# Three tiles instead of four beside the paged attention, token groups of 384 and 424, and a chunk inverse that multiplies half the columns

## The chip, the cores and the metric

The kernel runs on one core of a Trainium2 chip. The metric is the device time of one execution in microseconds, taken as the median of several runs. All arithmetic is in 32-bit floats. The engines are PE (matrix), DVE (vector), ACT (scalar), POOL (GpSimd), and SP, which here only issues DMA. PEld is PE's loading of weights. Each engine works through its own instruction list in order.

## The reference

One decoder layer for a prompt of 2048 tokens and a sample batch of 8 sequences of 4 tokens (32 rows, so 2080 tokens in all), width 1024. Cut to what matters here:

```
cols = rmsnorm(x) @ w_in           # columns split among three head groups
x += w_out @ concat[ GatedDeltaNet (6 heads of 64) | DiffAttention (4 heads of 64) | RWKV7 (6 heads of 64) ]
x += memory cross attention (4 heads of 128, 256 memory tokens)
x += ConvGLU: w_out @ (silu(causal conv3(gate)) * val),  gate, val = rmsnorm(x) @ w_in  (2816 each)
y = rmsnorm(x)
```

GatedDeltaNet works in chunks of 64 tokens: `a_mat` is strictly lower triangular, and `(a_mat + I)` has to be solved against `v` and `k` before the state is carried on. RWKV7 is a step by step recurrence on a 64x64 state per head; the kernel brings it to the same chunked form with a triangular inverse. The sample rows' DiffAttention reads a paged cache: 8 sequences x 64 pages x 128 positions of K and V, 512 pages each of 128 KB, found through a page table. The outputs are the final activations, the new K/V rows, and all states.

## The kernel before

`build` is a series of stages; within one stage several "lanes" run beside each other. A lane is one generator for each engine, and each `yield` in it is a slot. `weave` (L234) interleaves lanes by `(i + 0.5) / n` of slot i of n; `merge` (L243) interleaves them by places written out for each slot. The order it gives is the order in which the instructions stand in each engine's list, so an instruction that waits holds all of its engine's work behind it, whichever lane that is from.

The stages in order: `front` (norm, Q, K, V), then the input projection beside the prompt's DiffAttention, then the **paged stage**, then the sample rows' recurrences and the memory projection, then the **dense stage**, then the small outputs.

In the paged stage `paged_lanes` (162 slots: 16 for each of 8 sequences, 32 more for the last ones' remains, two others) runs beside the first LEAD = 4 tiles of 128 prompt tokens of `gdn_lanes` (24 slots a tile) and after them of `rwkv_lanes` (25 slots a tile), joined by `in_turn`. A third lane on SP, `states`, loads constants and states. In each of the first 128 paged slots PE flips one group of four K pages (L1190) for `score`; K has a ring of six groups, all loaded in the first slot on SP (L1136), one more each slot after that. V has a ring of seven groups of four pages, three pages issued by POOL and one by ACT, and is applied four groups at a time (L1249), at slots 5, 8, 11 and 14 of the sequence after. The last application is paged slot 143 in the lane's own count.

In the dense stage `feed_lanes` takes the 2080 tokens in NCH = 5 groups of CH = 416 (`op` output projection, `ns` norms, `wq`, `sc`, `tp`, `pv`, `wo` memory attention, `fg`, `fv`, `fo` feed-forward, `ft` turning back for the store; 129 slots a group). The other 12 tiles of both recurrences run beside it, three to a group in groups 0 to 3, spread over the first 0.92 of the group. SP waits in `tokens_done` for the tiles that the next group needs. The sample rows' memory attention, `memory_lanes`, runs beside group 4, which has no recurrence tile.

A recurrence tile has the slots `pre` to `RV` (GDN: to `X0`), then the chunk inverse, then `KS`, `SA`, `OD` for each of its two chunks, `post` and `back`. The inverse is `Scan64`. It keeps the inverse X and its transpose XT for 6 heads and 2 chunks of 64, and doubles the size of the inverted blocks at each of five levels b:

- slot `Y{b}`: `left` makes 12 products AM_b x X on PE, and ACT copies them to Y;
- slot `W{b}`: `right` makes 12 products for X (not at level 5) and 12 for XT, and DVE subtracts them from X and XT;
- POOL prepares the masked matrices AM_b.

All of these are 64x64 times 64x64, the two chunks in the two halves of the partitions. Each matmul stands in the trace as two instructions.

## Time and profile before

| | |
|---|---|
| median of 3 runs | 5926.58 us (5918.99 to 5926.8) |
| profiled execution | 5921.17 us, its span 5919.5 us |
| PE busy | 5294.7 us, 89% |
| PEld busy | 3261.9 us, 55% |
| DVE, ACT, POOL busy | 2368.5, 1498.2, 784.4 us (40, 25, 13%) |
| mean granted clock of PE | 0.917 of full speed |
| DMA | 487.80 MB, mean 82 GB/s |
| paged stage | about 1365 to 2180 us |
| dense stage | about 2440 to 5900 us |

Busy times are unions of an engine's instructions. The granted clock is the share of full speed that PE was given. A wait is idle time of an engine ahead of an instruction, with what ended it. The columns of the stage views are: stretch, its length, then busy time and number of instructions of PE, PEld, DVE, ACT and POOL (engines without such instructions are left out when one tile's name is asked for), PE's granted clock, the busy share of the DMA engines, and GB/s.

### The profile page before, as it was taken

What the parts mean: (1) busy time and instruction counts of PE and PEld (TensorE: products, weight loads), DVE (VectorE), ACT (ScalarE), POOL (GpSimd) and SP (SyncE); (2) the same over time, 40 slices, a digit from 0 to 9 for tenths busy, and PEclk for the clock granted to TensorE, in tenths of its full rate; (3) what the DMA queues carried; (4) which work ended last, traced back from release to release, by engine and by line L of the source; (5) the groups of instructions that cost most, each with busy time, mean ns of one, the idle gap of its engine ahead of it and who ended that gap; (6) DMA issues with size and microseconds to landing.
All of it is one profiled execution on the core that took longest, in us unless ns stands there. A gap on an engine that the chain in (4) does not pass through costs nothing. (4 is left out here: it accounts for less than half of the span.)

```text
span 5919.5 us, 91242 instructions
## 1 busy us (share of the span) xinstructions
PE 5294.7 (89%) x34908; PEld 3261.9 (55%) x34908; DVE 2368.5 (40%) x5479; ACT 1498.2 (25%) x3418; POOL 784.4 (13%) x1063
## 2 busy tenths in 40 slices
PE   8988999995777756889999899998999999989998
PEld 5644445554555542565555655565555655657554
DVE  1156655543445436253433534335333443321322
ACT  2235443432223210121212212122122221211212
POOL 0012221111443310110001101011010110100000
PEclk9989999997987855889999899998999989998998
DMA  3111011104776620312223122232233122241332
GB/s 97 48 31 36 29 33 35 35 32 137 227 223 193 181 70 9 105 43 72 86 72 102 51 73 84 77 84 62 73 87 93 54 76 74 75 130 51 95 94 69
DMA packets 729154, 487.80 MB, mean 82 GB/s; under 512 B 78058, under 2 KB 704106, under 8 KB 728687
## 3 DMA queue, kind: packets, MB, share of 16 engines
q1 hardware_dynamic: 677457, 393.53, 23.3%
q0 software_dynamic: 18432, 50.36, 2.9%
q10 hardware_dynamic: 32832, 38.09, 1.9%
q8 instruction: 278, 4.55, 0.3%
q14 instruction: 155, 1.27, 0.1%
HBM read 432.76 MB, written 49.09 MB: 81 GB/s over the span
## 5 line engine op out<-in xcount | busy, mean ns | idle before, releaser
L3368 PE MATMUL s_f_b<-s_f_h,s_f_W 128*128 128x416 f32 x4480 | 1640.8, 522 | 31.1 <-DMA s_f_h<-o_t 22.1
L3368 PEld LDWEIGHTS s_f_b<-s_f_h,s_f_W 128*128 128x128 f32 x4480 | 845.8, 192 | 708.7 <-issue 691.3
L3426 PE MATMUL s_f_b<-s_f_a,s_f_W 128*128 128x416 f32 x1760 | 634.1, 516 | 0.2
L536 PE MATMUL s_p_acc<-s_hT,s_p_W 128*128 128x416 f32 x1600 | 626.3, 539 | 6.9 <-DMA s_p_W<-in_w_in_dram 6.9
L3426 PEld LDWEIGHTS s_f_b<-s_f_a,s_f_W 128*128 128x128 f32 x1760 | 328.5, 190 | 263.5 <-issue 257.4
L536 PEld LDWEIGHTS s_p_acc<-s_hT,s_p_W 128*128 128x128 f32 x1600 | 300.1, 196 | 286.2 <-issue 269.5
L3624 DVE TENSOR_TENSOR s_f_xT<-s_f_xT,s_f_b 128x416 f32<-128x416 f32 x160 | 93.5, 586 | 587.1 <-PE s_f_b L3426 533.3
L3645 POOL TENSOR_TENSOR s_f_ex<-s_f_ex,s_f_mix 128x416 f32<-128x416 f32 x105 | 111.8, 1065 | 1348.9 <-ACT s_f_mix L3454 1348.3
L918 ACT ACTIVATE s_prob<-s_s_ps,s_ntop 128x512 f32<-128x512 f32 (+3 forms) x320 | 196.4, 619 | 368.2 <-DVE s_ntop L969 368.0
L3497 ACT ACTIVATE s_f_raw<-s_f_b 128x416 f32<-128x416 f32 x110 | 56.9, 517 | 774.9 <-PE s_f_b L3368 774.9
L1165 POOL DMA_DIRECT2D s_V<-in_cache_diff_v_dram x384 | 207.6, 541 | 278.5 <-issue 274.9
L966 DVE TENSOR_REDUCE s_ntop<-s_s_ps 128x2 f32<-128x1024 f32 (+3 forms) x160 | 169.9, 1062 | 62.8 <-PE s_s_ps L866 60.5
L3557 DVE TENSOR_SCALAR s_f_mix<-s_f_raw,s_f_taps,s_f_bias 128x416 f32<-128x416 f32 (+1 forms) x110 | 56.7, 516 | 321.8 <-ACT s_f_raw L3497 160.5
L1190 PE MATMUL s_tp<-s_ident,s_K 128*128 128x128 f32 x1024 | 162.9, 309 | 24.1 <-DMA s_K<-in_cache_diff_k_dram 17.6
L3507 ACT ACTIVATE s_f_val<-s_f_b 128x416 f32<-128x416 f32 x110 | 56.8, 516 | 444.1 <-PE s_f_b L3368 444.1
L866 PE MATMUL s_s_ps<-s_kT,s_qT 32*128 32x512 f32 (+3 forms) x640 | 163.4, 587 | 0.0
L1190 PEld LDWEIGHTS s_tp<-s_ident,s_K 128*128 128x128 f32 x1024 | 129.7, 158 | 41.2 <-DMA s_K<-in_cache_diff_k_dram 18.8
L1046 POOL TENSOR_SCALAR s_prob<-s_prob,s_alpha 128x512 f32<-128x512 f32 (+3 forms) x160 | 103.2, 660 | 275.5 <-DVE s_alpha L996 272.8
L1365 DVE COPY s_kT<-s_tp 128x512 f32<-128x512 f32 x128 | 88.2, 689 | 126.1 <-PE s_tp L1190 125.2
L1310 ACT ACTIVATE s_kT<-s_tp 128x512 f32<-128x512 f32 x128 | 75.9, 593 | 219.3 <-PE s_tp L1190 217.2
L1249 PE MATMUL s_o_ps<-s_V,s_PT 128*32 128x256 f32 x1024 | 82.0, 475 | 55.1 <-DMA s_V<-in_cache_diff_v_dram 55.0
L3171 POOL TENSOR_TENSOR s_g_zg<-s_g_zt,s_norm_g 128x384 f32<-128x384 f32 x16 | 16.0, 997 | 850.6 <-DVE s_g_o L3051 805.4
(790 smaller groups left out, 8010.0 us busy)
## 6 DMA issues: line engine op xcount, KB each, us to landing
s_f_W<-in_ffn_w_in_dram SPq DMA_DIRECT2D x220, 512.0 KB, 3.9
s_K<-in_cache_diff_k_dram SPq DMA_DIRECT2D x512, 128.0 KB, 2.9
s_V<-in_cache_diff_v_dram POOLq DMA_DIRECT2D x384, 128.0 KB, 3.2
s_f_W<-in_ffn_w_out_dram SPq DMA_DIRECT2D x80, 448.0 KB, 3.8
cols_t<-s_p_out ACTq DMA_DIRECT2D x100, 208.0 KB, 1.9
s_f_W<-in_w_out_dram SPq DMA_DIRECT2D x40, 512.0 KB, 4.6
s_f_W<-in_ffn_w_out_dram SPq DMA_DIRECT2D x40, 512.0 KB, 4.1
s_V<-in_cache_diff_v_dram ACTq DMA_DIRECT2D x128, 128.0 KB, 3.3
```

Source lines behind the costliest of these rows:

```text
L536: mm = pe.matmul(self.acc[n % 2][:, 0:CH], self.W[:, u, k, :], self.hT[:, k, c * CH:(c + 1) * CH], start=(k == 0), stop=(k == KD - 1))
L866: mm = pe.matmul(s_ps[hh][:, m, 0:wd], qT[r:r + 32, b, i * P:(i + 1) * P], kT[r:r + 32, b, 512 * c:512 * c + wd], start=True, stop=True)
L918: e = act.activation(prob[:, slot(n, c), r, 0:wd], s_ps[hh][:, m, 0:wd], ACT.Exp, scale=scale, bias=ntop[:, u, c, r:r + 1], accum_out=den[ ...
L966: dve.tensor_reduce(ntop[:, u, c, 2 * hh:2 * hh + 2], s_ps[hh][:, :, 0:wd], AX.X, ALU.max)\
L1046: m = pool.tensor_scalar(prob[:, k, 2 * hh + 1, 0:wd], prob[:, k, 2 * hh + 1, 0:wd], alpha[:, n % 2, c, 2 * hh + 1:2 * hh + 2], 1.0, ALU.m ...
L1165: pool.dma_start(V_[:, g % VG, i, :], vp[page_of(pool, g, i)].rearrange("a p h d -> p (a h d)"))\
L1190: mm = pe.transpose(dst[:, i, :], K[:, g % KG, i, h * P:(h + 1) * P], pr.ident[:, :])
L1365: dve.tensor_copy(kT[:, g % 6, 1, :], src[:, :, :].rearrange("p i n -> p (i n)"))\
L3368: mm = pe.matmul(bank(u)[:, 0:G], w[:, k, :], h[:, k, :], start=(k == 0), stop=(k == KD - 1 and kind != "op"))
L3426: mm = pe.matmul(bank(u)[:, 0:G], w[:, k, :], a[:, f % NA, :], start=(k == 0), stop=(k == len(part) - 1))
L3624: dve.tensor_tensor(xT[:, m, :], xT[:, m, :], bank(u)[:, 0:G], ALU.add).then_inc(E.sem[kind + "k"], 1)
L3645: pool.tensor_tensor(acc, acc, sq[:, m % 2, :], ALU.add).then_inc(E.sem["add"], 1)
```

## The change

Four edits that go together:

1. LEAD goes from 4 to 3: three tiles of each recurrence run in the paged stage, 13 in the dense stage.
2. The token groups are 384, 424, 424, 424 and 424 instead of five of 416. Group 0 needs exactly three tiles. `spread` gives each group the tiles that the next one needs: four pairs in group 0 and three in groups 1 to 3. The quarters of a group are 96 or 106 tokens.
3. `Scan64` multiplies only the half of the columns that a level changes: of each pair of blocks of 2^b columns `left` reads the left half of X, `right` the left half of Y and the right half of XT. The products stand packed in the PSUM bank (32 columns a head), and ACT's copy and DVE's subtractions work on 192 elements a partition instead of 384. The 64x64 operand that is loaded as weights stays whole.
4. Y gets a home of its own with a slice for each level, zeroed once by POOL, since only half of its columns are written: 1,920 elements a partition. In the paged stage it lies in the tile that later holds the memory's K and V, and both recurrences use it in turn.

```
-LEAD = 4
+LEAD = 3
+GROUPS = (384, 424, 424, 424, 424)
+GROUP_AT = tuple(sum(GROUPS[:c]) for c in range(len(GROUPS)))
+GROUP_P = GROUPS[-1] - NS
...
+    def side(self, x, r, h, b, right):
+        return x[r, h, :].rearrange("p (k a s) -> p k a s", a=2, s=2 ** b)[:, :, right, :]
+
+    def sides(self, x, b, right):
+        return x.rearrange("p h (k a s) -> p (h k) a s", a=2, s=2 ** b)[:, :, right, :]
+
+    def cell(self, bank, r, h, b):
+        return bank[r, h * HD // 2:(h + 1) * HD // 2].rearrange("p (k s) -> p k s", s=2 ** b)
+
+    def cells(self, bank, b):
+        return bank[:, 0:W_A // 2].rearrange("p (k s) -> p k s", s=2 ** b)
...
     def left(self, pe, bank, b):
         for h, r in self.each():
-            mm = pe.matmul(self.view(bank)[r, h, :], self.AM[b % 2][r, h, :], self.X[r, h, :], start=True, stop=True)
+            mm = pe.matmul(self.cell(bank, r, h, b), self.AM[b % 2][r, h, :], self.side(self.X, r, h, b, 0),
+                           start=True, stop=True)
         return mm
...
-                pe.matmul(self.view(bank_x)[r, h, :], self.XT[r, h, :], self.Y[r, h, :], start=True, stop=True)
-            mm = pe.matmul(self.view(bank_xt)[r, h, :], self.Y[r, h, :], self.XT[r, h, :], start=True, stop=True)
+                pe.matmul(self.cell(bank_x, r, h, b), self.XT[r, h, :], self.side(self.Y[:, b - 1, :, :], r, h, b, 0),
+                          start=True, stop=True)
+            mm = pe.matmul(self.cell(bank_xt, r, h, b), self.Y[r, b - 1, h, :], self.side(self.XT, r, h, b, 1),
+                           start=True, stop=True)
         return mm
+
+    def keep_y(self, act, bank, b):
+        return act.activation(self.sides(self.Y[:, b - 1, :, :], b, 0), self.cells(bank, b), ACT.Copy)
+
+    def less_x(self, dve, bank, b):
+        x = self.sides(self.X, b, 0)
+        return dve.tensor_tensor(x, x, self.cells(bank, b), ALU.subtract)
+
+    def less_xt(self, dve, bank, b):
+        x = self.sides(self.XT, b, 1)
+        return dve.tensor_tensor(x, x, self.cells(bank, b), ALU.subtract)
...
             if slot[0] == "Y":
+                if t == 0 and slot == "Y1":
+                    act.wait_ge(blank, 1)
                 need(act, T, slot, t)
-                go(inv.Y[:, :, :], inv.view(B[0]), ACT.Copy)
+                inv.keep_y(act, B[0], int(slot[1:])).then_inc(A.sem, 1)
...
                 if b < inv.LEVELS:
-                    dve.tensor_tensor(inv.X[:, :, :], inv.X[:, :, :], inv.view(B[1]), ALU.subtract)
-                tt(inv.XT[:, :, :], inv.XT[:, :, :], inv.view(B[2]), ALU.subtract)
+                    inv.less_x(dve, B[1], b)
+                inv.less_xt(dve, B[2], b).then_inc(V.sem, 1)
...
+        pool.memset(Y[:, :, :, :], 0.0).then_inc(blank, 1)
...
             if c:
                 E.wait(sp, "fv", c - 1, FB - 1)
-                C.tokens_done(sp, (c + 1) * G)
+                C.tokens_done(sp, GROUP_AT[c] + GROUPS[c])
...
-                    mm = pe.matmul(bank(u)[:, 0:G], w[:, k, :], h[:, k, :], start=(k == 0), stop=(k == KD - 1 and kind != "op"))
+                    mm = pe.matmul(bank(u)[:, 0:G], w[:, k, :], h[:, k, 0:G], start=(k == 0), stop=(k == KD - 1 and kind != "op"))
...
-                C.mK_T, C.mV = sb("mK_T", [P, MH, MEM]), sb("mV", [P, 2, MI])
+                mem_kv = sb("mem_kv", [P, MH * MEM + 2 * MI])
...
+                C.y_home = lambda st, name: mem_kv[:, 0:5 * 6 * HD].rearrange("p (b h d) -> p b h d", b=5, h=6)
...
                     def spread(lane):
                         per = lane.slots // (TILES - LEAD)
-                        return [t // 3 + 0.92 * ((t % 3) * per + k + 0.5) / (3 * per) for t in range(TILES - LEAD) for k in range(per)]
+                        places, t0 = [], LEAD
+                        for c in range(NCH - 1):
+                            t1 = min(-(-(GROUP_AT[c + 1] + GROUPS[c + 1]) // P), TILES)
+                            n = (t1 - t0) * per
+                            places += [c + 0.92 * (k + 0.5) / n for k in range(n)]
+                            t0 = t1
+                        return places
```

The remaining edits put the group's own width in place of the fixed 416 in every operation of `feed_lanes` and in `memory_lanes`.

## Rows read from the trace of the kernel before

**Rows 1.** The page: busy time, share of the span and instructions of each engine.

```profile
PE 5294.7 (89%) x34908; PEld 3261.9 (55%) x34908; DVE 2368.5 (40%) x5479; ACT 1498.2 (25%) x3418; POOL 784.4 (13%) x1063
```

**Rows 2.** Busy time by stretch: paged bulk, paged tail, dense groups 1 and 4.

```profile
1365.00:2106.00 741.00, 551.79 (x6815) 396.18 (x6813) 330.29 (x713) 185.86 (x352) 265.96 (x446) 0.83 0.66 195
2106.00:2180.00 74.00, 47.12 (x638) 40.65 (x638) 22.89 (x58) 7.71 (x18) 5.92 (x6) 0.59 0.01 2
...
3153.00:3866.00 713.00, 678.27 (x4995) 425.55 (x4995) 278.56 (x635) 162.49 (x347) 73.04 (x72) 0.96 0.27 76
...
5293.00:5900.00 607.00, 568.88 (x1890) 342.29 (x1890) 134.18 (x355) 112.56 (x266) 22.30 (x21) 0.92 0.31 89
```

**Rows 3.** The same by tile: s_shared (recurrences) in the bulk, s_f_b (dense) in both groups.

```profile
1365.00:2106.00 741.00, 229.30 (x4009) 188.69 (x4007) 93.45 (x228) 45.30 (x94) 0.83 0.66 195
...
3153.00:3866.00 713.00, 521.54 (x1542) 278.50 (x1542) 26.54 (x44) 46.87 (x107) 0.96 0.27 76
...
5293.00:5900.00 607.00, 523.13 (x1566) 295.46 (x1566) 26.55 (x44) 53.16 (x133) 0.92 0.31 89
```

**Rows 4.** PE's waits, 1365 to 2106 us (total, times, longest); last row 1400 to 1440.

```profile
PE s_o_ps L1249 <- DMA s_V<-in_cache_diff_v_dram: 48.8, 14, 7.7
PE s_shared L2394 <- DVE s_g_E L3051: 18.4, 3, 6.5
PE s_tp L1190 <- DMA s_K<-in_cache_diff_k_dram: 17.6, 7, 9.1
...
PE s_tp L1190 <- DMA s_K<-in_cache_diff_k_dram: 15.0, 4, 9.1
```

**Rows 5.** PE's waits in dense group 1, 3153 to 3866 us.

```profile
PE s_bank L2593 <- DVE s_r_o L2671: 9.9, 2, 5.0
```

**Rows 6.** SP's DMA issues in order of time, all K issues, and SP's waits there.

```profile
1351.95 0.39 SPq L2875 DMA_DIRECT2D s_g_cq<-cols_t  x1
...
1357.46 31.16 SPq L1136 DMA_DIRECT2D s_K<-in_cache_diff_k_dram  x28
...
1639.15 26.18 SPq L1136 DMA_DIRECT2D s_K<-in_cache_diff_k_dram  x24
...
L1136 SPq DMA_DIRECT2D s_K<-in_cache_diff_k_dram x512: 337/338/1627, 1357.5 to 2013.1; - x171
...
SPq L1129 <- PE s_tp L1190: 34.4, 17, 6.6
...
SPq L2472 <- ACT s_r_u L2604: 5.7, 1, 5.7
```

**Rows 7.** PE and PEld in order of time: start, length; stage start, tail, dense stage.

```profile
1363.52 2.93 PE L2901 MATMUL s_shared<-s_g_sq,s_ones_half 128*128 128x384 f32 x4 [23.51 <-DVE s_qd L1433]
...
2110.20 0.83 PE L2501 MATMUL s_shared<-s_ones_half,s_r_ksq 128*128 128x2 f32 x6
...
2124.78 0.49 PE L2405 MATMUL s_shared<-s_r_kp,s_r_Dx 64*64 64x64 f32 x4 [0.58 <-ACT s_r_kp L2604]
...
2128.87 1.54 PE L2399 MATMUL s_shared<-s_r_rs,s_r_G 64*64 64x64 f32 x24 [1.20 <-DVE s_r_Dx L2671]
...
2458.61 0.19 PEld L2906 LDWEIGHTS s_bank<-s_g_g,s_incl 64*64 64x64 f32 x4 [0.55 <-issue]
2458.72 0.20 PEld L2909 LDWEIGHTS s_bank<-s_g_g,s_ones 64*64 64x64 f32 x4
...
2523.34 0.33 PE L2405 MATMUL s_bank<-s_g_sq,s_g_E 64*64 64x64 f32 x4
...
2524.62 0.33 PE L2406 MATMUL s_bank<-s_g_E,s_g_sq 64*64 64x64 f32 x4
```

**Rows 8.** Groups of DVE and ACT, dense group 1: busy, mean ns, idle before.

```profile
L2671 DVE TENSOR_TENSOR s_r_Dx<-s_r_Dx,s_bank 128x384 f32<-128x384 f32 x15 | 8.2, 548 | 3.4 <-PE s_bank L2406 3.2
...
L2764 DVE TENSOR_TENSOR s_r_rhs<-s_r_rhs,s_bank 64x192 f32<-64x192 f32 x12 | 3.7, 352 | 4.9 <-PE s_bank L2568 4.9
...
L2604 ACT ACTIVATE s_r_kp<-s_bank 128x384 f32<-128x384 f32 x15 | 7.3, 488 | 20.0 <-PE s_bank L2399 20.0
```

More of the change, by code:

```diff
@@ L2435, in rwkv_lanes @@
     oT = st.sb("r_oT", [P, 3, P])
-    inv = Scan64(C.levels, C.eye, six(rs), six(Dx), six(kp), (six(G_), six(ep)))
+    Y = C.y_home(st, "r_Y")
+    blank = st.sem("r_blank")
+    inv = Scan64(C.levels, C.eye, six(rs), six(Dx), Y, (six(G_), six(ep)))
     B = [st.ps(f"r_b{j}", [P, 512]) for j in range(3)]
@@ L2850, in gdn_lanes @@
     six = lambda x: x.rearrange("p c (a d) -> p (c a) d", d=HD)
-    inv = Scan64(C.levels, C.eye, six(rs[:, 0:3, :]), E[:, :, :], six(rs[:, 3:6, :]), (gB[:, :, :], Eb[:, :, :]))
+    Y = C.y_home(st, "g_Y")
+    blank = st.sem("g_blank")
+    inv = Scan64(C.levels, C.eye, six(rs[:, 0:3, :]), E[:, :, :], Y, (gB[:, :, :], Eb[:, :, :]))
     B = [st.ps(f"g_b{j}", [P, 512]) for j in range(3)]
@@ L3030, in step @@
             if slot[0] == "Y":
+                if t == 0 and slot == "Y1":
+                    act.wait_ge(blank, 1)
                 need(act, T, slot, t)
-                go(inv.Y[:, :, :], inv.view(B[0]), ACT.Copy)
+                inv.keep_y(act, B[0], int(slot[1:])).then_inc(A.sem, 1)
             if slot == "post":
@@ L3216, in feed_lanes, with sub @@
     L = Lanes()
-    G, NA, RING = CH, 9, 4
+    GM, NA, RING = max(GROUPS), 9, 4
+    Q = GM // 4
     PARTS = (range(0, 8), range(8, 15), range(15, 22))
-    SUB = [(0, 104), (104, 104), (208, 104), (312, 104)]
-    LAST = [(0, 104), (104, 104), (208, 104), (312, 72), (384, NS)]
-    sub = lambda c: SUB if c < NCH - 1 else LAST
+    quarter = lambda c: GROUPS[c] // 4
+    def sub(c):
+        q = quarter(c)
+        if c < NCH - 1:
+            return [(i * q, q) for i in range(4)]
+        return [(0, q), (q, q), (2 * q, q), (3 * q, GROUP_P - 3 * q), (GROUP_P, NS)]
     plan = [("op", m) for m in range(8)] + [("gap", 0), ("ns", 0)] + [("wq", j) for j in range(4)] + [("gap", 1)]
@@ L3380, in step @@
                 free(pe, u)
-                pe.matmul(bank(u)[:, 0:G], pr.ones[:, :], acc, start=True, stop=True).then_inc(E.sem[kind], 1)
+                pe.matmul(bank(u)[:, 0:G], pr.ones[:, :], acc[:, 0:G], start=True, stop=True).then_inc(E.sem[kind], 1)
             if kind == "sc":
@@ L3416, in step @@
                 for k in range(MH):
-                    mm = pe.matmul(bank(u)[:, 0:G], w[:, k, :], qT[:, k, :], start=(k == 0), stop=(k == MH - 1))
+                    mm = pe.matmul(bank(u)[:, 0:G], w[:, k, :], qT[:, k, 0:G], start=(k == 0), stop=(k == MH - 1))
                 mm.then_inc(E.sem[kind], 1)
@@ L3425, in step @@
                         E.wait(pe, "act", c, f)
-                    mm = pe.matmul(bank(u)[:, 0:G], w[:, k, :], a[:, f % NA, :], start=(k == 0), stop=(k == len(part) - 1))
+                    mm = pe.matmul(bank(u)[:, 0:G], w[:, k, :], a[:, f % NA, 0:G], start=(k == 0), stop=(k == len(part) - 1))
                 mm.then_inc(E.sem[kind], 1)
@@ L3449, in square @@
                     E.wait(act, "ns", c, w - 1)
-                act.activation(acc, xT[:, m, :], ACT.Square).then_inc(E.sem["sq"], 1)
+                act.activation(acc[:, 0:G], xT[:, m, 0:G], ACT.Square).then_inc(E.sem["sq"], 1)
                 return
@@ L3472, in step @@
                 E.wait(act, "wq", c, j)
-                act.activation(qT[:, j, :], bank(u)[:, 0:G], ACT.Copy, scale=float(MHD) ** -0.5).then_inc(E.sem["qk"], 1)
+                act.activation(qT[:, j, 0:G], bank(u)[:, 0:G], ACT.Copy, scale=float(MHD) ** -0.5).then_inc(E.sem["qk"], 1)
             if kind == "sc":
@@ L3487, in step @@
                     E.wait(act, "tp", c, 2 * j + x)
[L3488 removed]
+                    act.activation(pT[:, x, :, 0:n], bank(u)[:, 0:GM].rearrange("p (h n) -> p h n", n=Q)[:, :, 0:n], ACT.Copy)\
                        .then_inc(E.sem["ptk"], 1)
@@ L3506, in step @@
                 E.wait(act, "act", c, j - 2)
-                act.activation(val[:, j % 2, :], bank(u)[:, 0:G], ACT.Copy).then_inc(E.sem["vk"], 1)
+                act.activation(val[:, j % 2, 0:G], bank(u)[:, 0:G], ACT.Copy).then_inc(E.sem["vk"], 1)
             if kind == "gap" and j == 7:
```

84 lines of the change are left out of this document (45 added, 39 removed).

## The prediction

> **What bounds the kernel now.** I read the page first. PE is busy 89% of the span, and the next engine, DVE, 40% [rows 1]; a saving elsewhere counts only where PE waits for it. Then the busy time by stage [rows 2], because the change moves work between two stages. In the paged stage (1365 to 2180 us) PE is busy 552 of the 741 us in which pages are read, at a mean clock of 0.83, and then comes a tail of 74 us in which almost only the last RWKV tile runs, at 0.59. In the dense stage each of groups 0 to 3 lasts 713 us, with PE busy 678 us at 0.96. So a recurrence tile leaves a stage where PE idles a quarter of the time and enters one where PE is nearly full.
>
> Next I split PE's time by tile names [rows 3] and its idle time by releaser [rows 4, 5]. In the 741 us the recurrences hold PE for 229 us, and the dense group without them 522 us. PE's idle time in the 741 us is 189 us: DMA of V 49, of K 18 (15.0 of it in one stretch, 1400 to 1440), and in some 25 small rows about 95 us at recurrence tiles, of which the largest is shown [rows 4]; the rest is the paged lane's waits for ACT and DVE. Last I read the DMA-issuing queue of SP [rows 6]. It issues 512 K pages between 1357.5 and 2013.1 us at (26.18 - 0.34) / 23 = 1.12 us each, 575 us together; some 60 other issues lie between them. It waits visibly only 34.4 + 5.7 = 40 us in that time. SP is hardly slower than PE here, and that caps the gain.
>
> **Part 1: one tile of each recurrence leaves the paged stage.** Slots are interleaved by (i + 0.5) / n. The recurrences have 4 x (24 + 25) = 196 slots now and 147 after; the paged lane keeps 162. When PE applies the last V pages (paged slot 143) it has passed 174 recurrence slots now, 130 after. The bulk loses 44 of 174: 229 x 44/174 = 58 us of PE work, and 95 x 44/174 = 24 us of waits.
>
> The start changes too, as the order of the first two slots turns round: 0.5/196 lies before 0.5/162, 0.5/147 behind it. On SP the first recurrence load now goes ahead of the page table and the pages [rows 6]. After, it stands behind the table and the 24 pages of the first paged slot: 24 x 1.12 = 27 us later. Queued behind its arrival are the `pre` operations of GDN on DVE, ACT and POOL, on ACT and POOL the K copies and V issues behind them, and on PE slot `n` and all flips after the first. PE's start moves from 1363.5 [rows 7] to about 1391. Meanwhile six groups of K arrive, so the 15.0 us wait for K at 1400 to 1440 goes; the net loss is 27 - 15 = 12 us.
>
> By PE alone the last V apply then ends at 2110.2 [rows 7] + 12 - 58 - 24 = 2040. By SP alone the last page is issued at 2013.1 - 40 (its waits) - 3 (five DMAs fewer) = 1970. From there to the last apply are 97.1 us now; 25 recurrence slots lie in it, 18 after, at (229 + 95)/174 = 1.9 us each, so it becomes 84 us and the end is 2054. The later one decides, and neither hides fully in the other (V waits of 49 us stay, as POOL still issues its V pages between recurrence operations). I take 2064: **46 us saved**. The bounds are 56 (2054) and 31 (the late start is not absorbed and the chain waits stay: 58 - 27).
>
> The tail: now 22 slots of the last RWKV tile follow the last apply, from `flip`; after, 17, from `W1`. That removes 2110.2 to the first W at 2124.8 [rows 7], 14.6 us. There the chunk inverse's chain is bare, and DVE's step between W and the next Y costs 1.20 us of PE idle [rows 7]. Two DVE operations of 548 ns become 192 elements wide; one of that width takes 352 [rows 8], so 0.4 us a level, 0.2 at level 5. ACT's copy (488 ns [rows 8]) I shorten by the same ratio, 0.15 us a level. Four levels and the last: 2.5 us. Tail **17 us saved**.
>
> **Part 2: that pair of tiles enters the dense stage.** PE's busy time of a group less that of the dense tiles is 678.3 - 521.5 = 156.7 us for three pairs [rows 2, 3], 52.2 a pair; PE idles for recurrence tiles 20 us in a group (half of it at L2593 [rows 5]), 6.7 a pair; sum 58.9. From the other side: group 4 has no recurrence; 607 us less the 568.9 - 523.1 = 46 of its memory lane is 561, so a pair costs (713 - 561)/3 = 51, because recurrences also fill holes of the dense work. Group 0 gets four pairs, 100 slots instead of 75 in 0.92 of the group, 6.7 us apart instead of 8.7; waits like that of `back` grow, which gives the upper bound 65. I take **57 us lost** (51 to 65).
>
> **Part 3: groups of 384 and four of 424.** Columns sum to 2080 as before, with the same number of instructions; the trace's 416-column matmul is a stream paced by its columns, so this is 0: 522 x 32/416 = 40 us less in group 0 and 10 more in each other. Bound: a nanosecond more or less on 6,560 instructions, 7 us.
>
> **Part 4: half the columns in the inverse.** A tile and lane issues 168 matmuls (336 instructions in the trace: 60 left and 108 right, twice), 26 x 336 = 8,736 in the dense stage. They are not shortened by half. In [rows 7] 44 instructions of 64 columns go from 2523.34 to 2524.62, 29.1 ns each. The nearest row with fewer columns is L2906, the same 64x64 weights with 6 columns: four go in 0.11 us, 27.5 ns each (26.3 to 28.8 with rounding). So the weight load, which stays 64x64, sets the pace, and 58 fewer columns buy 1.6 ns. At the tail's low clock L2399's 24 instructions last 1.54 us [rows 7], less the last one's own 0.3 some 53 ns each, and no row there prices fewer columns. I take the 1.6 ns: 14 us. The smaller DVE and ACT operations are covered in the dense stage by 6 us of dense matmuls between slots; without that cover they would be the tail's 2.5 us a tile. In the paged bulk SP sets the end, so nothing is counted. So **14 us saved** (0 to 24, for a pace between 29.1 and 26.3).
>
> The zeroing of Y runs once a stage on POOL while PE waits for its first load, 0. Merging the two memory tiles costs nothing.
>
> **Sum:** -46 - 17 + 57 - 14 = -20 us. The profiled execution took 5921.2 us (span 5919.5), 5.4 under the median of 5926.6; against the median this is 5907.
>
> **The rivals.** With B the saving in the paged bulk, the total is 26 - B. A measurement of this kernel tells some 0.2%, 12 us: faster needs B over 38, slower B under 14.
> 1. *Forecast*: B = 46, near 5907 (5889 to 5917). For it: SP and PE both have 40 to 80 us to give up. Against it: they meet. Chance 0.50.
> 2. *No change to tell*: B near 30 and the fourth pair dear (65): 5926.6 - 30 - 17 + 65 - 14 = 5931, or 5915 to 5923 with one of these alone. Speaking for it: the late start and 2 us tighter slots. Chance 0.24.
> 3. *Slower*: SP's issue is the bound already, and its 40 us of waits are replaced by others (the first load behind 24 pages, then a ring filled to the last slot by a PE that lags). Then K's last issue stays at 2013, and B is only the 13 us behind it: 5926.6 - 13 - 17 + 57 - 14 = 5940. It decides from B under 14. Against it: the waits recorded are for PE's flips, which come sooner with 58 us less work. Chance 0.13.
> 4. *The inverse does get its half*: if the pace of 64-column instructions were that of the columns, 8,736 x 14.5 ns = 127 us go: near 5794. L2906 speaks against it, but it is one group of four instructions. Chance 0.05.
> 5. *The paged stage isn't held by SP*: PE's own chain ends at 2040 and fewer adjacent recurrence slots remove more waits: B = 80, 5873. Chance 0.08.
>
> **How the numbers follow.** Faster by over 0.2%: cases 4 and 5 and nine tenths of case 1, 0.58. Slower: case 3 and a little of 2, 0.15. Within: 0.27. The likeliest case gives 5907. For the range, cases 1, 2 and half of 3 below, and most of 5 left out: 5880 to 5937; the likeliest case's own is 5889 to 5917.
>
> **What would show it.** The paged stage ends near 2117, its last V apply near 2064, SP's last K page near 1975 with waits under 10 us. The first recurrence matmul stands near 1391, behind the first flips. Group 0 lasts some 726 us, the next three 720. Right: L2405's successor still goes at 28 ns an instruction; wrong: under 25. The DVE operations of the inverse take 350 ns. The prediction fails if the last K issue doesn't move (case 3), if a pair costs over 65 us in group 0, or if the granted clock falls in the paged stage as PE has less to do there.

## The result and the profile after

The changed kernel takes 6091.68 us (median of 3 runs, 6086.76 to 6091.96) against 5926.58 before: a ratio of 1.0279 [1.0259, 1.0299], slower by 165 us. I had forecast 5907 us, and my range ended at 5937. In two of the kernels below one execution ran slow (6654.38 and 11688.51 us); it is left out of their medians and ratios. The changed kernel's line numbers are shifted by about 46 in the dense lanes; L2421 and L2423 are the right-hand products of the inverse, L2436 and L2432 its subtractions.

The page, first part (busy time, as [rows 1]):

```profile
PE 5348.2 (88%) x34908; PEld 3299.6 (54%) x34908; DVE 2310.7 (38%) x5479; ACT 1474.9 (24%) x3418; POOL 792.9 (13%) x1067
```

The same number of instructions keeps PE busy for 54 us more; the rest of the difference is idle time. Busy time by stretch, as [rows 2]: paged bulk, paged tail, then the five dense groups.

```profile
1365.00:2053.00 688.00, 491.90 (x5676) 339.85 (x5676) 278.00 (x606) 162.93 (x310) 246.50 (x418) 0.82 0.69 204
2053.00:2133.00 80.00, 45.24 (x619) 37.91 (x619) 16.69 (x43) 5.57 (x15) 13.11 (x21) 0.56 0.12 35
2389.00:3159.00 770.00, 712.08 (x6138) 481.68 (x6138) 307.06 (x762) 172.44 (x393) 87.89 (x90) 0.93 0.26 73
3159.00:3895.00 736.00, 689.61 (x5004) 429.14 (x5005) 268.87 (x635) 160.74 (x351) 73.70 (x72) 0.95 0.26 74
3895.00:4653.00 758.00, 703.54 (x4996) 438.98 (x4996) 268.91 (x635) 159.06 (x348) 74.08 (x72) 0.93 0.25 72
...
5411.00:6070.00 659.00, 586.63 (x1890) 351.51 (x1888) 135.62 (x355) 113.18 (x264) 22.69 (x21) 0.88 0.28 82
```

The paged stage went nearly as foreseen: the dense stage starts 50.7 us sooner, against the 63 that I had forecast. The dense stage lost that and far more. The best yardstick is where the first product of each group that adds x through the identity matrix (below: the identity product) stands, in us from the span's start, read from the view of that line; the differences are the lengths of the groups:

| kernel | dense starts | group 0 | 1 | 2 | 3 | 4, to the end |
|---|---|---|---|---|---|---|
| before | 2447.8 | 713.3 | 713.4 | 713.4 | 713.3 | 618.3 |
| after | 2397.1 | 769.7 | 736.0 | 757.8 | 757.7 | 671.7 |

I had said 726 us for group 0 and 720 for the next three. PE's waits in dense group 2 of after, 3895 to 4653 us (total, times, longest), where [rows 5] stood for before:

```profile
PE s_f_b L3414 <- issue: 12.7, 2, 6.3
PE s_bank L2624 <- DVE s_r_o L2704: 9.7, 2, 4.9
PE s_f_b L3482 <- ACT s_f_a L3567: 8.5, 1, 8.5
PE s_f_b L3419 <- DMA s_f_xs<-in_x_prompt_dram: 8.5, 1, 8.5
```

The wait for `back` (L2624) is as before. The other three are new: the output transposes (L3482) wait for ACT, the identity product (L3419) waits for x, and for the 12.7 us ahead of the output projection (L3414) the profile names no releaser. The first two lead to transfers. SP's issues between groups 1 and 2, in order of time (start, length), after:

```profile
3859.32 0.32 SPq L3354 DMA_DIRECT2D s_f_xs<-in_x_prompt_dram  x1
3859.68 5.36 SPq L3367 DMA_DIRECT2D s_f_h<-o_t  x1
3874.97 20.33 SPq L3385 DMA_DIRECT2D out_dram<-s_f_a  x4
...
3897.49 9.76 SPq L3354 DMA_DIRECT2D s_f_xs<-in_x_prompt_dram  x1
```

and the same place before:

```profile
3845.31 0.44 SPq L3308 DMA_DIRECT2D s_f_xs<-in_x_prompt_dram  x1
3845.79 0.42 SPq L3321 DMA_DIRECT2D s_f_h<-o_t  x1
3860.73 7.12 SPq L3339 DMA_DIRECT2D out_dram<-s_f_a  x4
...
3868.34 2.35 SPq L3308 DMA_DIRECT2D s_f_xs<-in_x_prompt_dram  x1
```

Issuing four stores of 106 rows takes SP 20.3 us where four of 104 rows took 7.1, and the load of x behind them takes 9.8 us to issue instead of 2.4. The windows of 4 us over the stores say why; the last two columns are the mean busy share of the 16 DMA engines and GB/s. First the kernel after, then the kernel before:

```profile
3879.00:3883.00 4.00, 0.00 (x0) 0.00 (x0) 0.00 (x0) 0.00 (x0) 0.00 (x0) 0.50 0.13 51
3883.00:3887.00 4.00, 0.64 (x3) 0.63 (x4) 0.00 (x0) 1.09 (x2) 0.00 (x0) 0.50 0.13 53
3887.00:3891.00 4.00, 1.31 (x7) 0.88 (x5) 0.00 (x0) 0.00 (x0) 0.00 (x0) 0.50 0.13 53
```

```profile
3862.00:3866.00 4.00, 2.77 (x16) 1.76 (x14) 0.00 (x0) 1.57 (x3) 0.00 (x0) 0.73 0.65 188
3866.00:3870.00 4.00, 2.87 (x5) 1.62 (x6) 0.00 (x0) 1.08 (x2) 0.00 (x0) 0.70 0.75 161
```

With 106 rows the stores run on 0.13 of the DMA engines, which is two of sixteen, at 51 to 53 GB/s, and PE is busy 2 of these 12 us: the four stores share two result buffers, so the third store's results can't be written before the first store has landed. By the Trainium skill, "DMA: Bandwidth & Descriptors", section "Why a DMA increments its semaphore by 16 and not by 1", a transfer uses the largest number of engines up to 16 that divides the slowest dimension of both its sides. Worked out from that page, this is 2 for 106 = 2 x 53, 13 for 104, 16 for 96 and 112. The trace agrees for 106 rows; for 104 it shows 0.65 and 0.75, where 13 of 16 would be 0.81 at most.

The inverse's products in dense group 0 of after, PE in order of time, against the same products in [rows 7]:

```profile
2474.07 0.29 PE L2423 MATMUL s_bank<-s_g_E,s_g_Y 64*64 64x32 f32 x4
2474.18 0.30 PE L2421 MATMUL s_bank<-s_g_Y,s_g_E 64*64 64x32 f32 x4
...
2475.00 0.30 PE L2423 MATMUL s_bank<-s_g_E,s_g_Y 64*64 64x32 f32 x4
```

From 2474.07 to 2475.00 go 32 instructions of 32 columns, 29.1 ns each: the pace of 64 columns in [rows 7]. Half the columns buy nothing on PE here.

### The profile page after: what moved, and what is told of

Its sections match the earlier page's. It is cut to its first block and busy times, and to the rows that moved or that the text cites. A ratio compares the mean times of both kernels' runs of the same rounds, so it can differ in the third digit from the quotient of the medians.

```text
span 6090.0 us, 91253 instructions
## 1 busy us (share of the span) xinstructions
PE 5348.2 (88%) x34908; PEld 3299.6 (54%) x34908; DVE 2310.7 (38%) x5479; ACT 1474.9 (24%) x3418; POOL 792.9 (13%) x1067
## 5 line engine op out<-in xcount | busy, mean ns | idle before, releaser
L3414 PE MATMUL s_f_b<-s_f_h,s_f_W 128*128 128x424 f32 (+1 forms) x4480 | 1649.5, 524 | 46.1 <-DMA s_f_h<-o_t 21.4
L3414 PEld LDWEIGHTS s_f_b<-s_f_h,s_f_W 128*128 128x128 f32 x4480 | 849.8, 193 | 726.1 <-issue 610.3
L3472 PE MATMUL s_f_b<-s_f_a,s_f_W 128*128 128x424 f32 (+1 forms) x1760 | 641.1, 521 | 0.0
L3672 DVE TENSOR_TENSOR s_f_xT<-s_f_xT,s_f_b 128x424 f32<-128x424 f32 (+1 forms) x160 | 93.7, 587 | 609.4 <-PE s_f_b L3472 539.5
L3693 POOL TENSOR_TENSOR s_f_ex<-s_f_ex,s_f_mix 128x424 f32<-128x424 f32 (+1 forms) x105 | 112.3, 1070 | 1405.5 <-ACT s_f_mix L3501 1405.0
L3544 ACT ACTIVATE s_f_raw<-s_f_b 128x424 f32<-128x424 f32 (+1 forms) x110 | 57.0, 518 | 771.3 <-PE s_f_b L3414 771.3
L3605 DVE TENSOR_SCALAR s_f_mix<-s_f_raw,s_f_taps,s_f_bias 128x424 f32<-128x424 f32 (+2 forms) x110 | 57.4, 522 | 311.3 <-ACT s_f_raw_s L3547 157.8
L3554 ACT ACTIVATE s_f_val<-s_f_b 128x424 f32<-128x424 f32 (+1 forms) x110 | 56.9, 517 | 459.8 <-PE s_f_b L3414 455.7
L3463 PE MATMUL s_f_b<-s_f_a,s_f_W 128*128 128x424 f32 (+1 forms) x320 | 129.7, 560 | 0.8 <-DVE s_f_a L3663 0.8
```

Of the source, the lines that this page charges most:

```text
L3414: mm = pe.matmul(bank(u)[:, 0:G], w[:, k, :], h[:, k, 0:G], start=(k == 0), stop=(k == KD - 1 and kind != "op"))
L3463: mm = pe.matmul(bank(u)[:, 0:G], w[:, k, :], qT[:, k, 0:G], start=(k == 0), stop=(k == MH - 1))
L3472: mm = pe.matmul(bank(u)[:, 0:G], w[:, k, :], a[:, f % NA, 0:G], start=(k == 0), stop=(k == len(part) - 1))
L3672: dve.tensor_tensor(xT[:, m, 0:G], xT[:, m, 0:G], bank(u)[:, 0:G], ALU.add).then_inc(E.sem[kind + "k"], 1)
L3693: pool.tensor_tensor(acc[:, 0:GROUPS[c]], acc[:, 0:GROUPS[c]], sq[:, m % 2, 0:GROUPS[c]], ALU.add).then_inc(E.sem["add"], 1)
```

## The experiments

Four theories run through them. A: rows of 106 (transfers). B: half the columns lower PE's granted clock. C or G: the group sizes themselves. F: the pair moved into the dense stage is dearer than 57 us. D, E and H are said in the expectations. Ratios are to runs of the kernel before on the same chip, with 95% intervals; 0.1% is 6 us. A ratio is not the quotient of the two medians and differs from it by up to 0.0014. A difference of two ratios is uncertain by some 0.0020 to 0.0035, 12 to 20 us.

Single profiles vary too. In the kernel before and in the three kernels at the end that change only the stage of the sample tokens, the dense code is the same; its group 0 took 713.3 us in two of their profiles and 719.7 in the other two, groups 1 to 3 713.3 to 713.5 in all four, and the last 618.2 to 628.8.

**Rows of 112 in the change.** Group of 424 as 112 + 112 + 112 + 88 instead of 4 x 106.

```diff
-    Q = GM // 4
+    Q = 112
-            return [(i * q, q) for i in range(4)]
+            return [(0, q), (q, q), (2 * q, q), (3 * q, GROUPS[c] - 3 * q)]
```

> The change with the groups of 424 tokens cut into rows of 112, 112, 112 and 88 instead of four times 106; nothing else differs. Theory A (transfers whose rows number 106 are moved badly: an output store took 20.3 us instead of 7.1, a load of x 9.8 instead of under 2.4, and TensorE waits for both at each group's start): most of the 110 us that groups 1 to 3 and the 54 us that the last group last longer come back, so 5940 to 6010 us, and the store is back near 7 us. Theory B (the half-width inverse makes TensorE idle more and its granted clock falls): no change beyond 10 us, 6080 to 6095. Theory C (the larger groups themselves, with more memory attention per group, cost this): no change either.

5982.1 us, ratio 1.0110 [1.0088, 1.0132]. Of 2.79% above before, 1.69% are gone: 100 us. Theory A holds for that much, and 65 us remain.

**Full columns in the change.** The old `left`, `right`, copy and subtraction; all else as changed.

> The change with the inverse over all 64 columns as in the kernel before; groups and lead stay as changed. Theory B (half the columns lower the activity and with it the granted clock, 0.93 to 0.95 against 0.96): 20 to 60 us come back, 6030 to 6070, and the clock of the dense windows is near 0.96. Theory A (rows of 106): no change, 6085 to 6105, since the instruction pace of the half columns was the same 29.1 ns.

6089.47 us, ratio 1.0288 [1.0264, 1.0313]: no change from 1.0279. The 20 to 60 us that B wanted back do not come. Perhaps the waits for the transfers cover them; no run shows it.

**Half columns alone, in the kernel before.**

> The kernel before with the half-width inverse alone (groups of 416, lead 4). My prediction's step said 14 us faster; after the trace of the change, whose 32-column products kept the pace of 29.1 ns, theory A says 0 to 10 us faster through shorter VectorE steps, 5916 to 5927. Theory B says slower: 20 to 60 us, with a lower clock in the first four groups, 5950 to 5990.

5951.27 us, ratio 1.0064 [1.0041, 1.0088]: slower by 38 us. Mean clock 0.907 to 0.911 over its runs, 0.918 to 0.922 in those of before. As B said, at the lower end of its range.

**Rows of 106 alone, in the kernel before.**

```diff
-    SUB = [(0, 104), (104, 104), (208, 104), (312, 104)]
+    SUB = [(0, 106), (106, 106), (212, 106), (318, 98)]
```

> The kernel before with its groups of 416 tokens cut into rows of 106, 106, 106 and 98 (106, 106, 106, 66 and 32 in the last) instead of 104; the fourth part of each x load is a load of its own. Theory A: each group's start waits for stores and loads again, 60 to 150 us slower, 5985 to 6075, and a store of 106 rows takes near 20 us. Theory B or C: within 20 us of before (the extra load costs under 2 us a group on SP).

6031.78 us, ratio 1.0193 [1.0169, 1.0218]: 114 us slower, with the old groups of 416 and one small load of x more for each of the eight. The row count costs this much without any change of group size. Groups last 727.1, 733.8, 734.0, 730.4 and 658.0 us.

**What is left of the change without both.** Rows of 112 and full columns: lead of three and the group sizes.

> The change with rows of 112, 112, 112 and 88 and with the old inverse over all 64 columns: what is left of the change is the lead of three tiles and the new group sizes. Theory D (each edit costs by itself, sums add up: half columns 33 us as measured alone): 5982 - 33 = 5949, against before 5918. Theory E (the half columns cost through the clock in stretches where TensorE already idles, and in the changed groups that is not worse): no gain over the run with rows of 112, 5975 to 5990. My prediction's own numbers for these parts (-46 - 17 + 57) give 5912, that is 6 us faster than before.

5957.97 us, ratio 1.0071 [1.0055, 1.0088]. Half columns cost 23 us here (1.0110 - 1.0071), give or take 16; that isn't told apart from the 38 alone. My own terms for this rest gave -6 us; it is +42.

**The same with a lead of four.**

```diff
-LEAD = 3
+LEAD = 4
```

> As the run above, but with LEAD = 4: four tiles of each recurrence beside the paged attention, as before, and groups of 384 and 424 with rows of 112. It tells the group sizes from the moved pair. Theory F (the fourth pair in group 0 costs some 90 us instead of 57, and the group sizes nothing): within 8 us of before, 5910 to 5926. Theory G (the group sizes cost by themselves): 5940 or more. Group 0 lasts about 680 us by F, since it has 384 tokens and three pairs, and no longer 770.

5915.98 us, ratio 0.9999 [0.9985, 1.0013]. The group sizes, in rows of 112, cost nothing that shows (8 us either way); the moved pair costs 43 us (1.0071 - 0.9999), give or take 13. The starts, with a lead of five from below:

| kernel (rows of 112, full columns) | dense starts | pairs in group 0 | group 0 | 1 | 2 | 3 | 4 |
|---|---|---|---|---|---|---|---|
| lead 3 | 2380.8 | 4 | 766.3 | 726.0 | 720.3 | 720.2 | 634.8 |
| lead 4 | 2431.8 | 3 | 681.2 | 725.7 | 726.6 | 720.4 | 634.9 |
| lead 5 | 2553.5 | 2 | 598.7 | 726.0 | 720.3 | 720.3 | 634.8 |

Group 0 whole, by busy time, lead 4 and then lead 3:

```profile
2431.80:3113.00 681.20, 645.73 (x4996) 427.64 (x4995) 273.44 (x635) 158.49 (x347) 72.17 (x72) 0.95 0.28 80
```

```profile
2380.80:3147.10 766.30, 709.00 (x6148) 480.23 (x6147) 320.93 (x760) 180.05 (x396) 86.78 (x89) 0.94 0.26 74
```

The fourth pair adds 63.3 us of PE's busy time and 21.8 us of idle time, 85.1 together. PE's waits in that group with a lead of three:

```profile
PE s_bank L2596 <- DVE s_r_o L2674: 20.1, 4, 6.0
PE s_bank L2397 <- DVE s_g_E L3054: 6.8, 1, 6.8
PE s_bank L2504 <- DVE s_r_ksq L2674: 6.5, 3, 4.1
```

With a lead of four the first is 10.9, the second 2.3 and the third 3.9 us, so these three rows account for 16 of the 21.8 us. Of the 63.3 us of busy time some is the clock: by the trace's clock record PE has 1.2 GHz for 96 us of group 0 with a lead of three and for 61 us with a lead of four. As an instruction takes 53 ns at 1.2 GHz against 29 at 2.4, these 34 us cost 16 at most; an estimate.

**Full columns on PE, half on DVE and ACT, in the kernel before.** The cut shows it against the kernel with half columns alone; `left` is one of three such products.

```diff
-pe.matmul(self.cell(bank, r, h, b), self.AM[b % 2][r, h, :], self.side(self.X, r, h, b, 0), ...)
+pe.matmul(self.view(bank)[r, h, :], self.AM[b % 2][r, h, :], self.X[r, h, :], ...)
-return dve.tensor_tensor(x, x, self.cells(bank, b), ALU.subtract)
+return dve.tensor_tensor(x, x, self.sides(self.view(bank), b, 0), ALU.subtract)
```

> The kernel before with the half-width inverse on VectorE and ScalarE only: TensorE's products go over all 64 columns again, the other two engines read half of them (strided). Theory B (fewer columns on TensorE lower its granted clock): the 33 us of the half-width inverse alone are gone, 5900 to 5920. Theory H (the shorter VectorE and ScalarE steps, or the strided reads, shift the interleaving and cost it): 5945 to 5955, as with half columns on TensorE.

5917.25 us, ratio 0.9999 [0.9987, 1.0011], clock 0.918 to 0.920. So the loss of half columns sits in PE's products, and on the whole the shorter DVE and ACT operations bring nothing that shows (7 us either way). Whether it is the number of columns or the strided way in which PE reads and packs them isn't told apart. The tail of the paged stage shows how the clock can come in. There the last RWKV tile runs bare, PE in order of time. Half columns:

```profile
2132.04 1.49 PE L2411 MATMUL s_shared<-s_r_rs,s_r_ep 64*64 64x32 f32 x24 [0.68 <-ACT s_r_rs L2632]
2133.96 0.43 PE L2418 MATMUL s_shared<-s_mem_kv,s_r_Dx 64*64 64x32 f32 x4 [0.43 <-ACT s_mem_kv L2425]
2134.19 0.41 PE L2420 MATMUL s_shared<-s_r_Dx,s_mem_kv 64*64 64x32 f32 x4
...
2136.33 0.42 PE L2420 MATMUL s_shared<-s_r_Dx,s_mem_kv 64*64 64x32 f32 x4
2137.56 1.49 PE L2411 MATMUL s_shared<-s_r_rs,s_r_G 64*64 64x32 f32 x24 [0.81 <-DVE s_r_Dx L2433]
2139.48 0.43 PE L2418 MATMUL s_shared<-s_mem_kv,s_r_Dx 64*64 64x32 f32 x4 [0.42 <-ACT s_mem_kv L2425]
...
2144.99 0.43 PE L2418 MATMUL s_shared<-s_mem_kv,s_r_Dx 64*64 64x32 f32 x4 [0.42 <-ACT s_mem_kv L2425]
```

Full columns, the same products of the same tile:

```profile
2118.12 1.54 PE L2405 MATMUL s_shared<-s_r_rs,s_r_ep 64*64 64x64 f32 x24 [0.68 <-ACT s_r_rs L2623]
2120.09 0.48 PE L2411 MATMUL s_shared<-s_mem_kv,s_r_Dx 64*64 64x64 f32 x4 [0.43 <-ACT s_mem_kv L2416]
2120.36 0.43 PE L2412 MATMUL s_shared<-s_r_Dx,s_mem_kv 64*64 64x64 f32 x4
...
2122.07 0.48 PE L2412 MATMUL s_shared<-s_r_Dx,s_mem_kv 64*64 64x64 f32 x4
...
2122.49 0.31 PE L2412 MATMUL s_shared<-s_r_Dx,s_mem_kv 64*64 64x64 f32 x4
2123.61 0.91 PE L2405 MATMUL s_shared<-s_r_rs,s_r_G 64*64 64x64 f32 x24 [0.81 <-DVE s_r_Dx L2424]
2124.94 0.34 PE L2411 MATMUL s_shared<-s_mem_kv,s_r_Dx 64*64 64x64 f32 x4 [0.42 <-ACT s_mem_kv L2416]
...
2128.74 0.34 PE L2411 MATMUL s_shared<-s_mem_kv,s_r_Dx 64*64 64x64 f32 x4 [0.42 <-ACT s_mem_kv L2416]
```

Both begin at 1.2 GHz and at one pace: 2.14 us from 2134.19 to 2136.33 for 40 instructions, 53 ns each, and 1.71 us from 2120.36 to 2122.07 for 32. Then the kernel with 64 columns rises to 2.4 GHz (the rows there shrink to 0.31 us and 24 instructions to 0.91), and its step from W to W takes 2128.74 - 2124.94 = 3.80 us. With 32 columns the granted clock reads 0.50 from 2132 to 2159 us and the step takes 5.51 us (2139.48 to 2144.99).

One pair of profiles would be weak evidence, since the kernel before has slow steps there as well. The length of `left`'s 24 instructions in the five steps of the last RWKV tile, in us (equal to 0.01 within a row; 1.54 and 1.49 are the pace of 1.2 GHz, 0.92 and 0.89 that of 2.4):

| kernel | columns | steps 1 to 5 |
|---|---|---|
| before; rows of 106 alone; one added product in the sample stage | 64 | 1.54, 1.54, 1.54, 0.92, 0.92 |
| three narrow added products in the sample stage | 64 | 1.55, 1.54, 1.54, 0.91, 1.55 |
| full columns on PE | 64 | 1.54, 0.91, 0.91, 0.91, 0.91 |
| lead 4; added products in the attention; three in the sample stage | 64 | 0.92 in all five |
| half columns alone | 32 | 1.49 in all five |
| lead 3, full columns, rows of 112, with and without added products | 64 | 0.92 in all five |
| lead 3, full columns, rows of 106 | 64 | 0.92, 0.92, 0.92, 0.92, 1.54 |
| after; after with rows of 112, or with stores or loads cut | 32 | 0.89, 0.89, 1.49, 1.49, 1.49 |

With 64 columns the chain climbs to 2.4 GHz or holds it to its last or last but one step; with 32 it stays at 1.2 GHz or falls back to it, in all five profiles. But from the first to the last of these `left` the kernel before took 23.0 us (2122.66 to 2145.64), half columns 22.1 and full columns on PE 16.9. So the five steps explain 5 us, and only against the faster of the two kernels with 64 columns.

The 34 us between the profiles of half columns and of full columns on PE lie so: the last V pages are applied 11.8 us earlier with full columns (2104.5 against 2116.3), the dense stage begins 26 us earlier (2430.4 against 2456.7), and its first four groups are 2 us shorter each (716 to 717 against 719). In these groups PE has 1.2 GHz for 290 us with half columns and for 253 with full ones, by the clock record. The start of the dense stage varies by 16 us between kernels with the same code up to there (below), so where the time goes is less sure than the 34 us themselves, which the ratios bear out over 5 and 10 executions. The groups of full columns on PE are also 3 us longer than the 713.4 of the kernel before: another part of the edit seems to cost that, and something earlier to make up for it; which, no run shows.

**Added products in the memory attention, in the kernel before.**

```diff
+                for _ in range(8):
+                    pe.matmul(bank((kind, c, 2 * j))[:, 0:P], pr.ident[:, :], pr.ident[:, :], start=True, stop=True)
                 E.wait(pe, "nrm", c, j)
```

> The kernel before with eight added 128x128 products of the identity ahead of each wait for the softmax in the dense groups' memory attention, where the granted clock falls to 0.79 to 0.91 and TensorE waits; their results are overwritten. They are 20 x 8 x 0.27 us = 43 us of TensorE's time if nothing hides them. Theory B (more activity there keeps the clock up): at most 10 us slower and the windows of 40 us in that part back above 0.9, perhaps 20 to 40 us faster. If the clock there does not depend on such activity: 30 to 45 us slower, 5950 to 5960, and the same clock.

5928.89 us, ratio 1.0019 [1.0006, 1.0031], mean clock 0.920 to 0.926. From 80 to 160 us into group 0 the granted clock reads 1.00 and 0.96, where before it reads 0.96 and 0.79. So 43 us of added work cost 11 (4 to 18): the rest fell into idle time or was given back by the clock. The clock can be moved there, but this way of moving it does not pay.

**Stores cut to n - 2 and 2 rows, in the change.** And, apart from it, **loads of x cut to 104 and 2 rows.**

```diff
-                    sp.dma_start(dst, res[0:n, j % 2, :]).then_inc(stored[j % 2], 16)
+                    cut = n - 2 if n > NS else n
+                    sp.dma_start(dst[0:cut, :] if n > NS else dst, res[0:cut, j % 2, :]).then_inc(stored[j % 2], 16)
+                    if n > NS:
+                        sp.dma_start(dst[cut:n, :], res[cut:n, j % 2, :]).then_inc(stored[j % 2], 16)
```

> The change, with each output store of n rows cut in two, n - 2 rows and 2 rows (106 as 104 + 2); x is still loaded in 106 rows. With rows of 106 throughout, group 1, which follows a store of 96 rows, lost 7 us against rows of 112, and groups 2 to 4, which follow stores of 106 rows, 31, 32 and 38 us. Theory A1 (the stores do it): some 75 of the 108 us come back, 6000 to 6025. Theory A2 (the loads of x do it): 6080 to 6095, since four more small stores a group cost nothing.

> The change, with each load of x in 106 rows cut into 104 and 2; the stores keep 106 rows. Theory A1: only 20 to 35 us come back, 6055 to 6075. Theory A2: most of the 108 us, 5985 to 6010.

Stores: 6014.7 us, ratio 1.0147 [1.0121, 1.0173], so 1.32% or 78 us come back, give or take 19. Loads: 6064.89 us, ratio 1.0238 [1.0216, 1.0259], 24 us, give or take 17. Together they match the 100 us that rows of 112 gave back, but part of that match is luck. The store edit also cut group 0's stores of 96 rows to 94 + 2, and 94 is 2 x 47: at the end of group 0, from 3164 to 3176 us, those stores run on 0.13 of the DMA engines at 51 to 52 GB/s, and group 0 lasts 785.6 us instead of 769.7. Without that the stores would have given back some 94 us, an estimate from these two lengths. The lengths of groups 0 to 4:

| kernel | group 0 | 1 | 2 | 3 | 4 |
|---|---|---|---|---|---|
| after | 769.7 | 736.0 | 757.8 | 757.7 | 671.7 |
| stores cut | 785.6 | 737.9 | 727.0 | 727.0 | 639.2 |
| loads cut | 769.6 | 736.1 | 747.4 | 747.6 | 668.2 |
| rows of 112 | 769.6 | 729.4 | 727.1 | 725.3 | 633.8 |

In groups 2 and 3 the stores alone bring the length to that of rows of 112; the loads of 106 rows cost their 10 us there only behind slow stores. So the two parts overlap, and the stores are the larger.

**Added products in group 0 alone, with a lead of three.** As with the added products above, but only for c == 0, in the kernel with rows of 112 and full columns.

> The run with full columns, rows of 112 and a lead of three (5958 us; group 0 lasted 766 us, of which 80 at a granted clock of 0.75 and 0.70), with eight identity products ahead of each softmax wait in group 0 alone: 4 x 8 x 0.27 = 9 us of TensorE's time. If the fourth pair is dear (85 us instead of 57) because the clock falls in that part: group 0 back to 745 to 755, time 5940 to 5950. If it is dear through VectorE, which the recurrences wait for: 5960 to 5967.

5950.95 us, ratio 1.0052 [1.0033, 1.0070] against 1.0071 [1.0055, 1.0088]: the intervals overlap. Group 0 lasts 769.9 us, 3.6 more, with 9 us of added work; in its poorest 80 us the clock reads 0.83 and 0.79 instead of 0.75 and 0.70. So a better clock in these 80 us gave back some 5 us. Group 0 didn't come down to the 745 to 755 us of the clock's side, and the time lies between the two ranges that I had given. How the pair's price divides between the clock and DVE's chains stays open.

**A lead of five.**

> The run with full columns and rows of 112, with five tiles beside the paged attention and eleven in the dense groups (two pairs in group 0, three in the others). By the traces a pair in the paged stage costs 51 us (5 of the dense start between leads of three and four, 2381 to 2432 us) and in group 0 the fourth costs 85. If the third costs as much as the predicted 52 to 57: no change against a lead of four, 5912 to 5925. If a pair is dearer in the dense stage wherever it goes (85): 5880 to 5895, faster than before. If the paged stage gets fuller and a pair costs more there: slower, over 5930.

5951.50 us, ratio 1.0049 [1.0027, 1.0072]: slower. Group 0 loses 82.5 us, as dear a pair as the fourth, but the paged stage grows by 121.7 us, where the fourth tile had cost it 51.0. Beyond four tiles that stage hides less of a tile's work.

**Added products in the stage of the sample tokens, in the kernel before.** One, three, and three narrow ones.

```diff
+                            for _ in range(3):
+                                pe.matmul(B[0][:, 0:P], pr.ident[:, :], pr.ident[:, :], start=True, stop=True)
                             pe.matmul(B[6 + i % 2][0:n, :], KR[...], S[...], start=True, stop=True).then_inc(T.sem, 1)
```

> The kernel before, and in the stage of the sample tokens one added identity product of 128x128 (128 columns) ahead of each of the 36 steps with products of 512 columns (24 on the states, 12 on the updates); nothing reads them. If the granted clock follows how much of the array the products fill: it rises above 0.50 in the run of 18.3 us that stood at 0.914 us a product, and 10 to 35 us are gained, less for VectorE, which is busy 63% there. If it does not rise: 36 x 0.43 = 15 us slower at most, nearer 5 where VectorE sets the pace.

> As the run before it, with three added products each. If use of the array decides: the clock is at 1.00 through the products of 512 columns, and the time is 0 to 30 us faster than before. If not: 36 x 3 x 0.43 = 46 us of added work, 20 to 46 us slower.

> As with three added products each, but narrow ones, 64 rows by 32 columns of the array with the same 128 moving columns. If use of the array decides: the clock stays at 0.50 in the run of 512-column products and the kernel is 20 to 46 us slower than before. If busy time alone decides: the same clock and time as with the three full ones.

5960.49 us, 1.0060 [1.0043, 1.0076]; 5982.44 us, 1.0113 [1.0094, 1.0131]; narrow 5941.14 us, 1.0030 [1.0019, 1.0042]. All are slower, by 36, 67 and 18 us, the first two by more than the 15 and 46 us that I had given as their most. The granted clock between 2220 and 2260 us and between 2300 and 2340 us is 0.50 and 0.50 before, the same with one and with three full products, and 0.63 and 0.71 with the narrow ones:

```profile
2220.00:2260.00 40.00, 29.16 (x127) 16.06 (x125) 26.84 (x38) 0.69 (x2) 0.00 (x0) 0.63 0.00 1
...
2300.00:2340.00 40.00, 31.65 (x177) 17.83 (x174) 24.43 (x34) 1.48 (x4) 0.00 (x0) 0.71 0.00 1
```

That is the reverse of what I expected from "use of the array". The theory falls in this form. What the clock follows stays open, and none of these kernels beats the one before.

## Why the prediction was wrong

Measured from differences of ratios: 1.0279 - 1.0110 for the rows, 0.9999 - 1 for the group sizes, 1.0071 - 0.9999 for the pair, 1.0110 - 1.0071 for the inverse, times 5920 us. The sum comes out by itself, since the four are steps of one chain of kernels; each step is uncertain by 8 to 18 us.

| term | predicted | measured |
|---|---|---|
| rows of 106 (within Part 3) | 0, bound 7 | +100 |
| group sizes 384 and 424 (Part 3) | 0 | -1 |
| Parts 1 and 2, the moved pair | -46 - 17 + 57 = -6 | +43 |
| Part 4, half columns | -14 | +23 (+38 alone) |
| sum | -20 | +165 |

**Part 3 failed, and it is most of the error.** I priced the groups of 424 as "a stream paced by its columns" and put the bound on PE's instructions alone. The matmuls did keep to that (a median of 486, 512 and 519 ns for 384, 416 and 424 columns). But the edit also changes every transfer that is shaped by the tile: four stores and eight loads of x a group go from 104 rows to 106. None of my rows was a transfer of the dense stage, and none of the rivals named one. The rule of the Trainium skill quoted above speaks against this part, and the prediction did not weigh it. That the time was lost there is shown both ways: 106 rows cost 114 us in the kernel before, 112 rows give 100 us back in the changed one, and stores and loads apart give 78 (with group 0's stores made slow) and 24.

**Part 2 was mis-sized**, 85 us instead of 57, above the bound of 65 beyond which I had said the prediction fails. Both of my derivations were averages: all recurrence work of a group over three, 52.2, and the length over a group without recurrences over three, 51. Both spread the holes of the dense work that the recurrences fill evenly over the pairs. The marginal pair in group 0 costs 82.5 us (third) and 85.1 us (fourth); of the fourth's, 63.3 is PE's busy time, where I had 52.2, and 21.8 idle time, where I had 6.7. That the first pairs fill the holes and leave none to the later ones fits these numbers; no run here shows it by itself. Also the idle time grows faster than the number of pairs: the four `back` waits take 20.1 us, where three took 10.9.

**Part 1 was nearly right.** In after the dense stage starts 50.7 us sooner, against my 63; in the pair of profiles with leads of three and four it is 51.0. SP's last K page is issued at 1990.3 us (I said 1975), the last V apply starts at 2077.6 (2064), and SP waits 22.5 us for PE's flips (I said under 10). The start was as described:

```profile
1353.31 0.26 SPq L1142 DMA_DIRECT2D s_table<-in_page_table_dram  x1
1355.57 26.07 SPq L1139 DMA_DIRECT2D s_K<-in_cache_diff_k_dram  x24
1381.68 0.44 SPq L2911 DMA_DIRECT2D s_g_cq<-cols_t  x1
```

The load stands behind 24 pages, at 1381.68 us instead of 1351.95 [rows 6], and the first recurrence product follows at 1387.66 (I said 1391). PE's waits in the bulk after, as [rows 4]:

```profile
PE s_o_ps L1252 <- DMA s_V<-in_cache_diff_v_dram: 50.2, 14, 9.6
PE s_tp L1193 <- DMA s_K<-in_cache_diff_k_dram: 29.8, 17, 3.6
PE s_shared L2937 <- ACT s_g_sq L3032: 24.2, 1, 24.2
```

The waits for V stay (48.8 before), the one for the late start is there with 24.2 us, but the waits for K grew from 17.6 to 29.8 us where I had let 15.0 of them go. These numbers are from one profile each, and the paged stage varies: kernels with the same code up to there started the dense stage at 2380.8, 2390.4 and 2397.5 us (lead 3, full columns), and at 2431.8, 2432.0, 2446.2 and 2447.8 (lead 4, full columns). The sum of the parts by the times (43) and by the profiles (85 - 51 = 34) agree within that.

**Part 4 had the pace right and the sign wrong.** The pace of 29.1 ns stands at 32 columns as at 64, and DVE's subtraction over 192 elements takes 349 to 354 ns, as said (350). The operations of the tail gained as said, too: at the pace of 2.4 GHz a step takes 3.80 us with the short operations against 4.36 in the kernel before, 0.56 where I had put 0.55. What I left out is that PE's granted clock can depend on the products' width. I named the clock among the things that would make the prediction fail, "in the paged stage as PE has less to do there", and gave it no price and no rival. It is shown that restoring whole columns in PE's products, with DVE and ACT left at half, brings the 34 us back. That the clock is the link is shown in the tail's timelines for some 5 us; for the rest it is argued from the time at 1.2 GHz and the mean clock (0.907 to 0.911 against 0.918 to 0.920). Why half columns cost nothing that shows with rows of 106 (1.0279 against 1.0288) and 38 us alone is open.

Of the rivals, case 3 had the sign, but for a reason that did not occur: SP's last K page moved from 2013.1 to 1990.3 us.

## What to carry to other kernels

When a tile size changes, price every transfer that takes its shape, not only the compute: its row count decides how many DMA engines carry it, and 106 rows cost a hundred microseconds here against 104 or 112. An edit that tests this changes row counts too: 96 rows cut to 94 fell into the same trap. Price a moved piece of work by what the last one of its kind adds to a stage, not by the stage's average; a second point (one tile more, one less) shows where the price changes: beside the paged pages the fourth tile cost 51 us and the fifth 122. A shorter instruction whose pace is set by something else gains nothing, and it can lose where the granted clock keeps changing between its two levels.
